# Running the first two output tiles of each normalised stage side by side, chunk by chunk

## The reference

```
h = rms_norm(x) * g * (1 + scale) + shift      # scale, shift: per channel, from a small matrix-vector product
y = h @ W                                       # W is 1024 x (512 to 5632)
```

## Time and profile before

| | us |
|---|---|
| median of 3 runs (2203.05 to 2204.77) | 2204.56 |
| the profiled execution: device time | 2202.74 |
| the profiled execution: span of its trace | 2200.9 |
| PE busy | 1945.0 (88%) |
| DVE busy | 1435.3 (65%) |
| ACT busy | 685.0 (31%) |
| POOL busy | 149.4 (7%) |

### The profile page before, as it was taken

The page is one execution under the profiler, slowest core; times in us unless marked ns, Lnnn a source line. Parts: engine busy times, 40 slices in busy tenths (PEclk is TensorE's granted clock), DMA queues, the critical chain, the costliest instruction groups (busy, mean ns, idle before and its releaser), DMA issues.

```text
span 2200.9 us, 26847 instructions
## 1 busy us (share of the span) xinstructions
PE 1945.0 (88%) x10068; PEld 1639.4 (74%) x10068; DVE 1435.3 (65%) x2081; ACT 685.0 (31%) x918; POOL 149.4 (7%) x73
## 2 busy tenths in 40 slices
PE   2971787779999998995899999989999998788998
PEld 2951787378888887884688888878888887568998
DVE  7877788787666667448866666676665227455554
ACT  2443343432222223223322222232222223244442
POOL 1000221020000010002200000100000010000000
PEclk9975798679999999998899999999999999799999
DMA  9830685033343443331333334433333224014444
GB/s 378 321 117 0 191 267 200 1 143 126 148 147 139 152 165 135 148 149 69 112 143 145 145 145 163 166 115 143 143 144 127 92 104 164 19 39 141 170 163 157
DMA packets 75731, 315.66 MB, mean 143 GB/s; under 512 B 19060, under 2 KB 22904, under 8 KB 56344
## 3 DMA queue, kind: packets, MB, share of 16 engines
q1 hardware_dynamic: 75136, 314.15, 39.9%
q10 hardware_dynamic: 536, 0.79, 0.1%
HBM read 313.86 MB, written 1.06 MB: 143 GB/s over the span
## 4 chain that ended last, share of the span: by engine, by line
PE 75%; DVE 15%; ACT 4%; issue 3%; DMA 1%; POOL 1%; SPq 0%; DVEq 0%; ACTq 0%
PE acc L1165 71%; DVE Wl L740 3%; PE psN L1165 2%; ACT Wh L501 2%; DVE tmp L727 2%; DVE psGT L772 1%; DVE psGT L769 1%; DVE psGT L775 1%; DMA afirst<-in_ada_w 1%; DVE XT L727 1%; PE psT L1265 1%; DMA raw<-in_odd_in 1%; DVE cy L727 1%; PE psN L1223 1%; DVE gates L1058 1%
## 5 line engine op out<-in xcount | busy, mean ns | idle before, releaser
L1165 PE MATMUL acc<-Hh,Wh 128*128 128x512 f32 (+1 forms) x2400 | 838.5, 349 | 106.8 <-DVE Hl L921 34.8
L1165 PE MATMUL acc<-Hl,Wh 128*128 128x512 f32 (+1 forms) x2400 | 832.5, 347 | 0.0
L1165 PE MATMUL acc<-Hh,Wl 128*128 128x512 f32 (+1 forms) x2400 | 831.9, 347 | 0.0
L740 DVE TENSOR_TENSOR Wl<-raw,Wh 128x2048 fp32r<-128x2048 f32 (+1 forms) x214 | 447.7, 2092 | 296.8 <-ACT Wh L501 296.7
L1165 PEld LDWEIGHTS acc<-Hh,Wh 128*128 128x128 f32 x2400 | 464.6, 194 | 172.5 <-issue 101.1
L1165 PEld LDWEIGHTS acc<-Hl,Wh 128*128 128x128 f32 x2400 | 464.8, 194 | 53.0
L1165 PEld LDWEIGHTS acc<-Hh,Wl 128*128 128x128 f32 x2400 | 464.2, 193 | 53.6
L501 ACT ACTIVATE Wh<-raw 128x2048 fp32r<-128x2048 f32 (+1 forms) x214 | 374.4, 1750 | 360.4 <-PE acc L1165 346.4
L1165 PE MATMUL acc<-hidh,Wh 128*128 128x512 f32 (+1 forms) x704 | 258.6, 367 | 0.9 <-DVE Wl L740 0.9
L1165 PE MATMUL acc<-hidl,Wh 128*128 128x512 f32 (+1 forms) x704 | 258.3, 367 | 0.0
L1165 PE MATMUL acc<-hidh,Wl 128*128 128x512 f32 (+1 forms) x704 | 258.2, 367 | 0.0
(11 more groups left out here) (198 smaller groups left out, 1064.9 us busy)
## 6 DMA issues: line engine op xcount, KB each, us to landing
raw<-in_ffn_up SPq DMA_DIRECT2D x88, 1024.0 KB, 4.7
graw<-in_mod_w SPq DMA_DIRECT2D x144, 512.0 KB, 5.4
raw<-in_ffn_down SPq DMA_DIRECT2D x64, 704.0 KB, 4.1
graw<-in_ada_w SPq DMA_DIRECT2D x32, 512.0 KB, 5.5
raw<-in_odd_in SPq DMA_DIRECT2D x16, 1024.0 KB, 4.9
raw<-in_even_in SPq DMA_DIRECT2D x12, 1024.0 KB, 5.8
raw<-in_conv_in SPq DMA_DIRECT2D x12, 1024.0 KB, 4.7
afirst<-in_ada_w SPq DMA_DIRECT2D x8, 1024.0 KB, 13.1
```

Of the source, the lines that this page charges most:

```text
L740: nc.vector.tensor_tensor(Wl[:, half, 0:f], raw[:, slot, 0:f], Wh[:, half, 0:f].bitcast(f32), ALU.subtract)\
L1165: return nc.tensor.matmul(out, lhsT, rhs, start=start, stop=stop)
```

## The change

In the eight normalised stages PE takes tiles 0 and 1 together: for each chunk the 6 matmuls of tile 0 and then the 6 of tile 1. PE waits for the low weights of both tiles before it starts, and for every accumulator to be free. Tile 0 is reported done at its last matmul in the last chunk, and tile 1 six matmuls later. The other tiles run in the loop as before. Nothing is changed on any other engine.

```diff
                     last.then_inc(tile_done, 1)
-                tiles(pe, s, SPLIT, 0, step, head=1 if s.drained0 == 0 else 0)
+                if s.name in NORMS:
+                    pe.wait_ge(lo_ready, s.n0 + 2)
+                    if s.drained0 > 0:
+                        pe.wait_ge(drained[s.by], s.drained0)
+                    for k in range(KC):
+                        pe.wait_ge(h_ready, H0[s.name] + k + 1)
+                        for t in range(2):
+                            for j in range(2):
+                                last = three(acc[t][j][:, 0:s.tokens], t, j * KC + k, Hh[:, k, c], Hl[:, k, c], k == 0, k == KC - 1)
+                            if k == KC - 1:
+                                last.then_inc(tile_done, 1)
+                    with pe.Fori(1, s.tiles // SPLIT) as i:
+                        for u in range(SPLIT):
+                            step(i * SPLIT + u, u, i)
+                else:
+                    tiles(pe, s, SPLIT, 0, step)
                 if s.name in ("even_in", "odd_in"):
```

## The result

| | us |
|---|---|
| before, median of 4 runs beside it (2202.37 to 2204.77) | 2203.81 |
| after, median of 4 runs (2257.39 to 2263.86) | 2259.34 |
| ratio, with its 95% interval | 1.0255 (1.0238 to 1.0273) |
| the profiled execution after: device time, span | 2257.39, 2255.6 |

The changed kernel is slower by 55.5 us; the profiled executions stand 2257.39 - 2202.74 = 54.65 apart. The forecast was 2256 (a sum of 52.4 more), the range 2236 to 2267.

A forecast was written before the change was run, and what follows sets the result against it. PE was taken to bound the kernel (busy 88% of the span). Gaps of 36.4 us plus clock loss of 16.0 make 52.4 on the profiled 2202.74: 2255.1, given as 2256, range 2236 to 2267.

The forecast's parts named there:

- The gaps: Before tile 2 in each of eight stages, PE idles once for its weights: 36.4 us lost in all.
- gqa_q: In this stage the 4 us gained in the pair are given back before tile 2: 0.4 lost, between -0.6 and 0.9.
- the subtraction: Before tile 2: loss is the weights' chain from tile 0's end plus 0.25, minus six matmuls, 0.72 or 1.36 us.
- The clock: Behind each of eight gaps PE restarts slowly: 2.0 us each, 16.0 in all (10.4 to 21.2).
- The order of matmuls: In the pair no matmul is added or taken away; unrolling 96 matmuls in seven more stages costs nothing.
- Nothing is taken back later: In the tiles after the gaps, PE's later waits recover nothing of the loss.
- All of these shift along: Waits in even_in (2.84 us) and odd_in (12.14 us) are tied to the tiles and move with them, recovering nothing.
- with a whole tile before it is needed, as now: Tile 4's load is delayed as much as tile 2's Wl, but still has a whole tile to spare.
- the second gap: Rival: tile 3's weights also come late, up to about 2 us in each of eight stages: 2275; chance 0.08.
- the clock stays up: Rival: PE keeps its clock in the gaps, so only 36.4 us are lost: 2239; chance 0.09.
- the delays taken up later: Rival: later PE waits absorb the delays of even_in, odd_in and ffn3_up, 20 us: 2236; chance 0.08.
- faster: Rival: tile 1 fills PE's waits and tile 2's weights are in time, at best 21.0 us gained: 2182; chance 0.03.

The follow-up runs named there:

- Experiment 2: The changed kernel with only the first four chunks of tiles 0 and 1 side by side: 2226.42 us, ratio 1.0101.
- experiment 4: Ffn up stages make the weights of the tile two on earlier, before hidh and hidl: in the changed kernel 2242.80 us, in the kernel before 2195.05.
- Experiment 5: The kernel before with the pair in gqa_q alone and a third weights place: 2203.98 us; also with earlier weights in ffn up: 2195.03.
- Experiment 1: The changed kernel with 34 to 48 unused matmuls between pair and tile 2 in each of the eight stages: 2246.82 us, ratio 1.0198.
- experiment 3: The kernel before with the pair in odd_in alone: 2216.25 us; the changed kernel with odd_in as before: 2249.23 us.
- experiments 1 and 6: 6: kernel before, earlier ffn up weights, gqa_q pair with third place, its Wh behind the norm's chunks, tile 3's split one step earlier: 2198.37 us.

## Why the prediction was right

- **The gaps.** From the last matmul of the pair to tile 2 it is 4.63, 4.63, 6.14, 4.55, 6.14, 6.13, 4.43 and 5.71 us; less one step of PE, that is 4.5, 4.5, 5.9, 4.3, 5.9, 5.9 and 5.6 for the stages other than gqa_q, as worked out. Experiment 2 changed the one term of the subtraction, experiment 4 the other, and both came out; in experiment 4 another wait took over after 1.7 of 2.1 us.
- **gqa_q.** The pair gained (its last matmul starts 13.1 us after the stage, before 17.6), and all of it went into the wait for tile 2, which starts 17.51 us after the stage against 17.75: -0.2, in the range of -0.6 to 0.9. With the clock's 1.5 the stage cost 1.2 instead of 2.4. Experiment 5 shows that it was the weights' place that took it: with a third place tile 2 starts 13.41 us after the stage.
- **The clock.** Tile 2 took 1.55 (even_in), 1.55, 2.35, 1.53, 2.44, 2.39, 1.48 and 2.29 us longer than before, 15.6 in all against 16.0. 2.0 for each was too much in four stages and too little in the other four, and the errors cancelled; that the sum came so near is luck. In the other profiles with the pair the same gap cost even_in or odd_in 1.3 to 2.8. One reading behind the 2.0 was wrong: the idle time just before the first tiles was not longer than 2.84 us everywhere, but 1.73 in even_in and odd_in, with short matmuls ahead of it; and even_in's first tile lost its 1.40 at a recorded clock of 1.00, which stays unexplained. Experiment 1 shows the mechanism: same gaps, clock 1.00, and the extra length gone. The Trainium skill ("TensorE: Matmul & The Clock Gate", HAM oscillation — how this bites in real kernels) advises to do all contraction steps of one tile before a wait, so that PE keeps its clock. The trace agrees for all eight gaps (0.50 to 0.64 behind them).
- **The order of matmuls.** Cost nothing, as said: with the gap at 0.44 us conv_in was 0.2 us shorter. The first two tiles of the stages of 512 tokens were even 0.3 to 0.8 us faster than before (23.3 to 23.4 us from the first to the last matmul), but the same pair took up to 24.5 in experiment 1, so no gain is shown.
- **Nothing is taken back later.** In even_in two things cancelled. Its pair began more slowly by 1.2 us (in kernels without that pair its start varies by up to 1.0), and later the wait of 2.84 us, which cost 1.3 us of clock before, came again without doing so. The pair alone does not decide that: of the seven profiles with the pair in even_in four kept the clock behind this wait and three lost it, as did all seven without:

```profile
102.07 0.35 PE L1165 MATMUL acc<-Hh,Wh 128*128 128x256 f32 x1 [2.84 <-DVE Wl L740]
```

- **The step that failed: "All of these shift along", for odd_in.** I had written of the raw loads "with a whole tile before it is needed, as now". Five of them landed late: ACT waited 12.7 us for them instead of 0.9, and PE four times. Its 16 tiles took 13.2 us more, where gap and clock make 6.1; the attention behind took 3.1 less, at a clock of 0.76 instead of 0.69 in stretches of 65 and 67 us:

```profile
391.00:456.00 65.00, 45.16 (x230) 25.16 (x229) 50.16 (x142) 34.03 (x104) 0.00 (x0) 0.76 0.08 31
```

```profile
372.00:439.00 67.00, 47.71 (x224) 25.88 (x222) 49.24 (x140) 34.01 (x104) 0.00 (x0) 0.69 0.07 27
```

(The second is the kernel before.) Those 3.1 us need not be the pair's doing: this attention, from the last matmul of the 16 tiles to the first of odd_out, is 62.4 to 63.8 us long in six of the 14 profiles, two of them without the pair in odd_in, and 65.2 to 66.0 in the others. So a part of the agreement of forecast and measurement is luck. The excess comes with the pair in odd_in (experiment 3) and varies: odd_in grew by 3.9, 7.3, 14.3, 7.8, 4.0 and 8.2 us in the six other profiles with that pair, by -2.6 to 0.8 in the six without; its 16 tiles alone by 4.0, 7.2, 14.3, 10.6, 6.3 and 10.0, against -0.1 to 2.7. The chance that I gave to something of this kind, the second gap, named the wrong cause: tile 3's weights were in time everywhere. What makes the loads land late stays open. SP issued the loads for tiles 4 and 5 closer together, at 286.99 and 291.91, 4.9 us apart where it was 5.8 before, and those for tiles 5 to 9 then took 8.6 to 11.2 us to land instead of 6.4 to 7.9. But in experiment 1 the two were as close, the loads of tiles 5 to 9 took 6.6 to 8.4 us, and odd_in had no excess, so the closer issue alone is not enough.

The rivals: the clock stays up (2239) falls with the 0.50 to 0.64 behind the gaps, the delays taken up later (2236) with the table, the second gap (2275) with tile 3, before which PE has no idle time in any of the eight stages, and faster (2182) with the gaps.

## To carry to other kernels

When two tiles are run together, ask not what the pair costs but when the first one's buffers come free: with two places, the third tile now waits for the whole refill chain minus what is left of the pair. Write that chain down instruction by instruction; shortening it in the kernel before, where one stage waited for it at every second tile, is what beats both kernels (ratio 0.9957, 2195.05 us). And where a stage loads its weights just in time, a delay of some microseconds inside it may not be neutral, as odd_in shows: the slack of each load has to be read, not assumed.

## What the runs showed of the hardware

- The same idle time did not always cost the clock. Behind the 2.84 to 2.87 us at the same place of even_in the granted clock was 0.50 to 0.72 in ten of the 14 profiles and 1.00 in four. Behind 1.68 us it stayed three times, behind 1.73 it fell, behind 1.85 it stayed, behind 2.00 and 2.19 it fell. After 4.35 it was still up at the restart and fell 0.8 us later.
- The attention after gqa_q has two lengths: 84.5 to 85.3 us, or 88.7 in the two profiles where a stretch of it stood at 0.93 and 0.94 instead of 1.00. That is enough to eat a true gain of 2.2 us or a third of what the fill gave back. It went with the kernels of experiments 1 and 6; what triggers it is not known.
- The loads of odd_in's raw weights took longer in the changed kernel: the median from issue to landing was 7.4 us before (274 to 316) and 8.8 after (285 to 335), with the DMA engines busy throughout (DMA share 1.03 and 0.96), while they moved 297 and 262 GB/s.
